# Solve products of a chunk pair issued as one group, alternating in row half and PSUM bank

## The reference

```python
m_low = jnp.where(strict, jnp.einsum('nbhik,nbhjk->nbhij', kb, k) * decay, 0.0)
rhs = jnp.concatenate([v * beta[..., None], kb * jnp.exp(G)[..., None]], axis=-1)
sol = lax.linalg.triangular_solve(m_low + jnp.eye(c, dtype=jnp.float32), rhs,
                                  left_side=True, lower=True, unit_diagonal=True)
...
def step(S, xs):
    qc, kc, uc, wc, Gc, ac = xs
    v_new = uc - jnp.einsum('bhck,bhkv->bhcv', wc, S)
    ...
```

## Time and profile before

| | us |
|---|---|
| median of 3 runs (lowest to highest) | 1933.58 (1927.35 to 1936.32) |
| the profiled execution's own time | 1931.35 |
| its span, first to last instruction | 1929.5 |
| TensorE busy in the span | 1816.6 (94%) |
| VectorE, ScalarE, GpSimd busy | 615.4, 510.2, 345.0 |
| mean granted TensorE clock | 0.968 of full |

### The profile page before, as it was taken

One profiled execution on the slowest core, in us unless ns is written; L12 is line 12 of the kernel. 1 busy time (PEld: TensorE's weight loads), 2 busy tenths in 40 slices (PEclk: granted clock), 3 DMA queues, 4 the chain that ended last, 5 costly groups with the idle time before them and its releaser, 6 DMA issues.

```text
span 1929.5 us, 34931 instructions
## 1 busy us (share of the span) xinstructions
PE 1816.6 (94%) x14904; PEld 1520.1 (79%) x14904; DVE 615.4 (32%) x1244; ACT 510.2 (26%) x1148; POOL 345.0 (18%) x246
## 2 busy tenths in 40 slices
PE   7999979999699998699999999999999999999997
PEld 4666645666588888456667779999999999999997
DVE  6542536511144444422314434111111111111145
ACT  3212563221144442201114314300330033003311
POOL 1010000000121211000010002333443333333530
PEclk9999999999799998899999989999999999999998
DMA  4010100100323210830013001111111111111202
GB/s 148 33 35 22 34 29 30 37 33 28 55 39 73 39 22 21 323 128 1 16 50 132 1 0 34 44 44 43 49 50 41 47 43 43 43 43 44 87 14 77
DMA packets 52334, 100.22 MB, mean 52 GB/s; under 512 B 7744, under 2 KB 34736, under 8 KB 51952
## 3 DMA queue, kind: packets, MB, share of 16 engines
q1 hardware_dynamic: 51168, 96.25, 15.7%
q0 software_dynamic: 1040, 2.12, 0.4%
HBM read 90.18 MB, written 7.58 MB: 51 GB/s over the span
## 4 chain that ended last, share of the span: by engine, by line
PE 54%; DVE 2%; POOL 2%; ACT 1%; issue 0%; DMA 0%; POOLq 0%; DVEq 0%; ACTq 0%
PE ps L1890 12%; PE ps L1891 12%; PE ps L1892 12%; PE ps L1768 11%; PE ps L1873 1%; PE ps L1738 1%; PE ps L1802 1%; PE ps L1731 1%; PE ps L1747 1%; POOL feat_r L1712 1%; PE ps L1814 0%; PE ps L1826 0%; POOL regH_r L1714 0%; PE ps L1721 0%; DVE feat L2197 0%
## 5 line engine op out<-in xcount | busy, mean ns | idle before, releaser
L1890 PE MATMUL ps<-feat_r,rows_r 128*128 128x352 f32 x1392 | 452.5, 325 | 9.9 <-DVE feat_r L2255 8.1
L363 PE MATMUL ps<-regH,regW 128*128 128x352 f32 x1296 | 392.4, 462 | 2.6 <-DVE regH L733 2.6
L363 PEld LDWEIGHTS ps<-regH,regW 128*128 128x128 f32 x1296 | 246.2, 191 | 139.9 <-issue 4.6
L1892 PE MATMUL ps<-feat_r,regW_r 128*128 128x352 f32 x1080 | 347.8, 322 | 0.0
L1890 PEld LDWEIGHTS ps<-feat_r,rows_r 128*128 128x128 f32 x1392 | 262.8, 189 | 11.5 <-issue 8.9
L1891 PE MATMUL ps<-regH_r,rows_r 128*128 128x352 f32 x768 | 247.1, 322 | 0.0
L1892 PEld LDWEIGHTS ps<-feat_r,regW_r 128*128 128x128 f32 x1080 | 203.9, 189 | 0.0
L1891 PE MATMUL ps<-feat_r,rows_r 128*128 128x352 f32 x624 | 201.3, 323 | 0.0
L2063 ACT ACTIVATE feat<-ps 128x352 f32<-128x352 f32 x96 | 44.6, 465 | 486.1 <-PE ps L1892 486.1
L2255 DVE TENSOR_TENSOR feat_r<-feat,feat_r (+1 forms) x96 | 55.1, 575 | 307.0 <-ACT feat_r L2067 307.0
L1891 PEld LDWEIGHTS ps<-regH_r,rows_r 128*128 128x128 f32 x768 | 144.9, 189 | 0.3 <-issue 0.2
(11 more groups left out here) (426 smaller groups left out, 2579.0 us busy)
## 6 DMA issues: line engine op xcount, KB each, us to landing
regW<-w_ff_in SPq DMA_DIRECT2D x45, 512.0 KB, 3.4
regW<-w_in_in SPq DMA_DIRECT2D x27, 512.0 KB, 3.5
regA<-xT_in SPq DMA_DIRECT2D x6, 1408.0 KB, 15.9
regA<-scr SPq DMA_DIRECT2D x80, 96.0 KB, 3.6
ext<-w_ff_in SPq DMA_DIRECT2D x15, 512.0 KB, 3.5
yT_out<-regA SPq DMA_DIRECT2D x12, 352.0 KB, 2.4
feat<-cv_in SPq DMA_DIRECT2D x8, 512.0 KB, 14.6
regH<-ck_in SPq DMA_DIRECT2D x8, 512.0 KB, 7.2
```

The lines of the kernel that those rows point to most:

```text
L363: ins = pe.matmul(ps[b][:, 0:BW], ring[n % 3][:, k * P:(k + 1) * P], hv[:, k, blk(b)], start=(k == 0), stop=(k == KT - 1))
L1890: pe.matmul(bank[:, 0:BW], hi, rhs_hi(k, b), start=(k == 0), stop=False)
L1892: ins = pe.matmul(bank[:, 0:BW], lo, rhs_hi(k, b), start=False, stop=(k == KT - 1))
```

## The change

U, X and P of both chunks of a pair are issued in one call. TensorE waits for both chunks first, and then the 12 products alternate between the banks ps0 and ps1: in each head pair p first c0's half 0 and c1's half 1, then c0's half 1 and c1's half 0. The two semaphores are counted up by the last product of c0 and the last of c1, which are the last two of the group. The token transposes K and M2 use the same order over ps3 and ps4. A last chunk that has no partner (the sample tokens) is issued alone, in the order p, h as before.

```diff
--- before.py
+++ after.py
@@ -1160,6 +1160,23 @@
                             ins = pe.matmul(bank[64 * h:64 * h + w, p * CW:(p + 1) * CW], m[e, p, :], ident[e, e], start=True, stop=True)
                     return ins
 
+                def crossed(pair, products):
+
+                    for p in range(NP):
+                        for n in range(2):
+                            for v in range(len(pair)):
+                                e = heads_()[(v + n) % 2]
+                                out, lhs, rhs = products(pair[v], e, p)
+                                ins = pe.matmul(out, lhs, rhs, start=True, stop=True)
+                                if p == NP - 1 and n == 1:
+                                    yield pair[v], ins
+
+                def both(c, k):
+
+                    if c % 2 and k <= levels(c - 1):
+                        return []
+                    return [x for x in (c, c + 1) if x == c or x <= NSEQ and k <= levels(x)]
+
                 def C_(j):
                     for c in range(*early[j]):
                         at = (c - early[j][0]) * 15
@@ -1189,31 +1206,39 @@
                     turned(ps[2], MT[c % 4]).then_inc(sem("Ttr"), 1)
 
                 def U_(c, k):
-                    v = c % 2
-                    if k == 0:
-                        pe.wait_ge(sem(f"t0{v}"), c // 2 + 1)
-                        if c >= 2:
-                            pe.wait_ge(sem(f"u{v}"), uv(c - 2, L))
-                    else:
-                        pe.wait_ge(sem(f"pd{v}"), ev(c, k))
-                    turned(ps[v], T_[c % 4]).then_inc(sem(f"Up{v}"), 1)
+                    pair = both(c, k)
+                    for x in pair:
+                        v = x % 2
+                        if k == 0:
+                            pe.wait_ge(sem(f"t0{v}"), x // 2 + 1)
+                            if x >= 2:
+                                pe.wait_ge(sem(f"u{v}"), uv(x - 2, L))
+                        else:
+                            pe.wait_ge(sem(f"pd{v}"), ev(x, k))
+                    for x, ins in crossed(pair, lambda x, e, p: (full(ps[x % 2])[e, p, :], T_[x % 4][e, p, :], ident[e, e])):
+                        ins.then_inc(sem(f"Up{x % 2}"), 1)
 
                 def X_(c, k):
-                    v = c % 2
-                    pe.wait_ge(sem(f"u{v}"), uv(c, k - 1))
-                    triple(ps[v], MT[c % 4], T_[c % 4]).then_inc(sem(f"Xp{v}"), 1)
+                    pair = both(c, k)
+                    for x in pair:
+                        pe.wait_ge(sem(f"u{x % 2}"), uv(x, k - 1))
+                    for x, ins in crossed(pair, lambda x, e, p: (full(ps[x % 2])[e, p, :], MT[x % 4][e, p, :], T_[x % 4][e, p, :])):
+                        ins.then_inc(sem(f"Xp{x % 2}"), 1)
 
                 def P_(c, k):
-                    v = c % 2
-                    pe.wait_ge(sem(f"x{v}"), ev(c, k))
-                    triple(ps[v], U[c % 4], X[v]).then_inc(sem(f"Pp{v}"), 1)
+                    pair = both(c, k)
+                    for x in pair:
+                        pe.wait_ge(sem(f"x{x % 2}"), ev(x, k))
+                    for x, ins in crossed(pair, lambda x, e, p: (full(ps[x % 2])[e, p, :], U[x % 4][e, p, :], X[x % 2][e, p, :])):
+                        ins.then_inc(sem(f"Pp{x % 2}"), 1)
 
                 def K_(c):
                     if c:
                         pe.wait_ge(sem("kw"), c)
                         pe.wait_ge(sem("mvb"), c)
-                    turned(ps[3], qkv[:, 3:6, tokens(c)], W(c))
-                    turned(ps[4], qkv[:, 6:9, tokens(c)], W(c)).then_inc(sem("tok"), 1)
+                    *_, (_, ins) = crossed((3, 4), lambda b, e, p: (full(ps[b])[e.start:e.start + W(c), p, :],
+                                                                    qkv[e, (b - 2) * 3 + p, tokens(c)], ident[e, e]))
+                    ins.then_inc(sem("tok"), 1)
 
                 def R_(c):
                     pe.wait_ge(sem("kq"), 2 * c + 2)
@@ -1252,8 +1277,9 @@
 
                 def M2_(c):
                     pe.wait_ge(sem("kv"), c + 1)
-                    turned(ps[3], zml[:, 3:6, tokens(c)], W(c))
-                    turned(ps[4], zml[:, 6:9, tokens(c)], W(c)).then_inc(sem("tokm"), 1)
+                    *_, (_, ins) = crossed((3, 4), lambda b, e, p: (full(ps[b])[e.start:e.start + W(c), p, :],
+                                                                    zml[e, (b - 2) * 3 + p, tokens(c)], ident[e, e]))
+                    ins.then_inc(sem("tokm"), 1)
 
                 def M3_(c):
                     pe.wait_ge(sem("qw"), c + 1)
```

## The result

The changed kernel takes 1967.0 us (median of 4 runs, 1966.3 to 1970.3) where the kernel before, on the same chip, takes 1935.0 (4 runs, 1927.4 to 1938.5). The ratio is 1.0174, with a 95% interval of 1.0141 to 1.0208: slower by 1.7%. The forecast was 1957.

What follows compares the result with a forecast made beforehand. TensorE was taken as the bound, busy 28.3 of 30 us mid-stage. 1931.35 + 25 (24 from eight pairs, 1 from the first) = 1956, or 1959 from the median; forecast 1957, 73% for 1946 to 1968, 8 in 10 for 1942 to 1982.

Steps and rivals of the forecast that it cites:

- Groups of 24 rows at 0.70: Solve groups and K, M2: in the crossed order 24 rows still take 0.70 us, 29 ns a row.
- The rival by which two banks speed TensorE up: 24-row groups: alternating banks free the halves; at 0.35 us a group the kernel ends near 1900 us; chance 7%.
- The rival of slower groups: Groups take 1.04 us each because rows start strictly in program order: about 2010 us; chance 3%.
- Two signals at 0.70, copies back to back: c0's result comes after 0.70 us, not 0.35; the two copies run together, 0.53 us on ScalarE, 0.63 on VectorE.
- The rival of no change: c0's products end early, so its copy starts as now and most waiting is hidden: about 1934 us; chance 8%.
- The joint wait: TensorE's next group waits for both copies: a part takes at least 1.54 us through ScalarE, 1.64 through VectorE.
- What hides it: Fill work on TensorE covers the wait in some parts; the rest lose 3.0 us a pair, 24 us in eight pairs.
- The first pair at half clock: +1: Three parts of the first pair run at half clock and lose a little more: +1 us, an estimate.
- The rival of the falling clock: Mid-stage, thinner TensorE work lowers the granted clock once a pair: +10 us, about 1967 us; chance 9%.
- Instruction stops fall into the new waits, up to 6 less: Stalls on instruction issue in the solve coincide with the added waits: up to 6 us less, 1951 us.
- The bounds for 8 in 10: 1942 us if one in three extra waits is hidden, 1982 us if clock and late fills come together.
- the late fills: Fills' own copies, queued behind the pair's, come late in two parts a pair: 5 us more, 1962 us.

Runs made afterwards that it cites:

- own_waits: The changed kernel with each chunk's wait placed at that chunk's own first product instead of both ahead of the group: 1955.6 us.
- joint_late: The changed kernel with its joint waits and late count, but products in the old order, all of c0's and then all of c1's: 1970.2 us.
- one_bank: The changed kernel with both chunks' products in the two halves of one PSUM bank, both readers waiting for the last product: 1971.7 us.
- late_signal: The kernel before, old order and separate waits, with only c0's semaphore counted up late, by c1's fifth product of six: 1942.2 us.
- first_pair_apart: The changed kernel with the first pair's solve groups issued per chunk as before, the other seven pairs grouped: 1960.8 us.
- the joint wait alone: The changed kernel's pairing and joint waits, but products in the old order, c0's six then c1's six, so c0's count comes early: 1962.5 us.

## Why the prediction was right

The sign, the place and the mechanism held, and 1967 lies in the range of 1946 to 1968, 1 us from its end; the forecast was 10 us short. By its own steps:

- **Groups of 24 rows at 0.70.** Right, in ten of the eleven traces at the full clock; in own_waits c1's wait holds the group in its middle. The rival by which two banks speed TensorE up falls to joint_late and one_bank, and so does the rule weighed there: the Trainium skill, TensorEngine Tiling, Gotcha 1: PSUM Pressure, would forbid what one_bank does at full rate (and the kernel before, with each half on its own 64 partitions). The rival of slower groups falls with the same rows.
- **Two signals at 0.70, copies back to back.** Right: 0.55 and 0.64 us in one piece. late_signal measures this alone at 8 us of solve, 2.8 of it in the first pair. The rival of no change, by which c0's products end early, falls with the copies' start, 0.90 to 0.96 us after the group's.
- **The joint wait.** Right in kind, short in size. A part was put at 1.54 and 1.64; it is 1.65 and 1.73. The term that was mis-sized is the hand-over back to TensorE, 0.05 in the sum. It is 0.14, from 656.91, where the second copy ends, to P1's first row at 657.05: the second wait of a product is an instruction of its own (51 ns), one of the 121 more of the page, and stands between the copy and the first weight load. That two waits would stand in front of one product was plain from the order; I priced them as one. The two copies, 0.55 in place of 0.53, are the rest.
- **What hides it.** The fill does, as listed: X2 to P2 1.77, U2 to X3 1.81, U4 to X5 1.74, U5 to the next U0 2.73, within 0.1 of before. Nine parts and X5 to P5 (2.58) each carry the 0.1 that the chain was short: the ten grew by 3.9, not by 3.0. That the pair still came out at 30.6 against the forecast 30.4 is luck: X4 to U4 shrank from 5.52 to 4.84, since the stop of 0.48 that stood in the earlier trace rows is missing from the pair after. The seven pairs behind the first lost 24.3 together where the forecast gives 21.
- **The first pair at half clock: +1.** Wrong by the most: the first pair lost 7.8 where the forecast gives 3 + 1. I saw the 0.50 in the earlier trace rows and took its end as given. It is not: with the groups that wait it came at 538 and not at 527 us, and with the first pair as before (first_pair_apart) 8.2 us of that pair came back.
- **The rival of the falling clock.** In the middle it didn't come: 1.00 from 545 to 750 us, and the fall that the earlier trace rows show at 588 is gone too. What the clock did lay at the stage's start, where it rose late.
- **Instruction stops fall into the new waits, up to 6 less.** They went from 3.9 to 2.9 in all.
- **The bounds for 8 in 10.** They don't follow from the terms named with them: 1957 less a third of 24 is 1949, not 1942, and 1967 for the clock with 5 for the late fills is 1972, not 1982.

The sum of the measured terms: 7.8 + 24.3 + 2.8 at the stage's start is 34.9, for 35.0 between the two profiled executions; the 10 us over the sum of 1956 are 3.8 of the first pair, 3.3 of the others and the 2.8, which the change did not make. Between the medians, 1935.0 and 1967.0, the change is 32 us where the sum has 25.

Do the two causes add? In a part without fill they nearly do: U0 to X1 takes 0.94 us before, 1.27 with the late count, 1.38 with the joint wait and 1.59 with both, so +0.33, +0.44 and +0.65. In the solve the late count alone costs 8.0 us, the joint wait alone 28.0, both 32.1; but 6.7 of the 28.0 are stops, by their difference to before. With each trace's own stops taken off, which is an estimate, the three are 8.9, 21.3 and 33.1.

## What to carry to other kernels

Here two chains on one engine covered each other because each had its own wait and its own early count; before merging such chains, cost one part as products + copies + hand-overs in a row, and see which parts have other work to hide it. The second wait in front of one product cost an instruction of its own (51 ns) here, and the hand-over grew from 0.05 to 0.14 us in each part where nothing covered it. This stage begins at half clock, and the change that thinned TensorE's work there moved the moment at which the clock rises from 527 to 538 us: cost such a beginning apart from the steady state.

## What the runs showed of the hardware

TensorE's stops without a wait lie at multiples of 256 instructions of its program (64 of 64, one remainder) and end 2.2 to 3.0 us after a 16 KB program transfer starts; the sum ranges from 1.5 to 11.3 us in a solve of 215 to 257, and what sets it stayed open. Rows of 64 x 64 products keep 29 ns apart at the full clock in every order of halves and banks that was tried, with both halves and both chunks in one bank too.
